# The Conformer convolution layer: projection in three one-pass products, and the depthwise convolution split between band matmuls on TensorE and taps on VectorE

## The reference, cut to what matters

```python
h = rms_norm(x, a_norm)
u = h @ w_in + b_in                       # 1024 -> 2048
a, gate = split(u, 2)
u = a * sigmoid(gate)
u = depthwise_causal_conv(u, w_dw) + b_dw # 31 taps in time, each channel by itself
u = silu(layer_norm(u, ln_g, ln_b))       # over the 1024 channels
x = x + u @ w_out + b_out
x = x + hierarchical_moe(rms_norm(x))     # then shared K/V, dilated attention, second MoE
```

## Time and profile before

| | us |
|---|---|
| median of 3 runs | 1848.68 (1848.21 to 1849.09) |
| the profiled execution's own time | 1853.51 |
| its span, first to last instruction | 1851.7 |
| TensorE, VectorE, ScalarE, GpSimd busy | 1562.5, 1170.6, 702.0, 509.6 |
| mean granted TensorE clock | 0.912 of full speed |

### The profile page before, as it was taken

How to read it: one execution, slowest core, us unless ns; L and a number is a source line. 1 busy time by engine, 2 the same in 40 slices (tenths; PEclk the granted TensorE clock), 3 DMA queues, 4 the chain that set the end, 5 groups by cost and what they waited for, 6 DMA issues and landing times. The chain is left out here.

```text
span 1851.7 us, 19289 instructions
## 1 busy us (share of the span) xinstructions
PE 1562.5 (84%) x6688; PEld 1171.9 (63%) x6688; DVE 1170.6 (63%) x1426; ACT 702.0 (38%) x762; POOL 509.6 (28%) x430
## 2 busy tenths in 40 slices
PE   6868048499999993799999999999998569999992
PEld 3323027367776662688888888888887556667760
DVE  2999992565666653848576574766643575656653
ACT  3323441245546551442232323323232335555541
POOL 2677700222222322314042240413310022322220
PEclk8988569589999996899999999999999679999996
DMA  3430000248887874212021211212111647888854
GB/s 151 188 136 21 25 0 30 114 162 356 356 364 324 341 310 186 93 58 70 32 81 55 68 57 45 79 45 69 55 57 70 288 150 294 343 371 350 368 228 158
DMA packets 44846, 303.08 MB, mean 164 GB/s; under 512 B 9488, under 2 KB 10256, under 8 KB 30992
## 3 DMA queue, kind: packets, MB, share of 16 engines
q1 hardware_dynamic: 34304, 284.98, 39.0%
q0 software_dynamic: 9648, 16.80, 2.5%
q10 hardware_dynamic: 864, 0.94, 0.1%
HBM read 295.34 MB, written 25.69 MB: 173 GB/s over the span
## 5 line engine op out<-in xcount | busy, mean ns | idle before, releaser
L626 POOL TENSOR_TENSOR KQ<-rope_ab 64x512 f32<-64x512 f32 x96 | 172.6, 1798 | 431.7 <-DVE rope_ab L1223 428.1
L1132 DVE TENSOR_TENSOR wgl<-WR,wgh 128x2048 fp32r<-128x2048 f32 x66 | 148.2, 2288 | 175.7 <-ACT wgh L741 172.8
L1404 PE MATMUL PS<-WR,SC 128*128 128x512 f32 x528 | 233.2, 594 | 4.1 <-ACT SC L775 3.2
L807 ACT ACTIVATE wh<-wraw 128x1024 fp32r<-128x1024 f32 x80 | 84.4, 1058 | 276.2 <-PE PS L1460 253.1
L1404 PEld LDWEIGHTS PS<-WR,SC 128*128 128x128 f32 x528 | 98.8, 190 | 118.3 <-issue 116.4
L1306 PE MATMUL PS<-HT,WR 128*128 128x512 f32 x256 | 123.5, 647 | 36.0 <-DVE SC L917 34.0
L928 DVE SCALAR_TENSOR_TENSOR SC<-SC 128x512 f32<-128x512 f32 x144 | 153.2, 1134 | 0.0
L1132 DVE TENSOR_TENSOR wul<-WR,wuh 128x2048 fp32r<-128x2048 f32 x66 | 148.0, 2283 | 0.3 <-ACT wuh L741 0.3
L741 ACT ACTIVATE wgh<-WR 128x2048 fp32r<-128x2048 f32 x66 | 122.4, 1904 | 62.0 <-DMA WR<-w_gate 62.0
L741 ACT ACTIVATE wuh<-WR 128x2048 fp32r<-128x2048 f32 x66 | 122.7, 1906 | 31.1 <-PE PS L1378 20.7
L1223 DVE TENSOR_TENSOR rope_ab<-PS,rope_sb 32x512 f32<-32x512 f32 x192 | 131.9, 687 | 2.6
(11 more groups left out here) (245 smaller groups left out, 3322.4 us busy)
## 6 DMA issues: line engine op xcount, KB each, us to landing
WR<-w_gate SPq DMA_DIRECT2D x33, 2048.0 KB, 12.3
WR<-w_up SPq DMA_DIRECT2D x33, 2048.0 KB, 16.8
WR<-w_down SPq DMA_DIRECT2D x33, 2048.0 KB, 14.0
wraw<-w_qkv SPq DMA_DIRECT2D x72, 512.0 KB, 3.3
WR<-w_in SPq DMA_DIRECT2D x8, 1024.0 KB, 4.8
WO<-w_out SPq DMA_DIRECT2D x1, 4096.0 KB, 14.8
xn_dram<-HTQ SPq DMA_DIRECT2D x8, 512.0 KB, 2.6
HT<-y_dram SPq DMA_DIRECT2D x8, 512.0 KB, 6.5
```

The source lines that it names most:

```text
L626: ins = nc.gpsimd.tensor_tensor(dst[h][0:HEAD, g, :], rope_ab[rows, 2 * (t % 2), :], rope_ab[rows, 2 * (t % 2) + 1, :], ALU.add)
L1132: V.tensor_tensor(lo[:, kts, :], raw[:, kts, :], hi[:, kts, :].bitcast(F32), ALU.subtract).then_inc(done, 1)
L1404: ins = M.matmul(PS[3 + h][:, :], hidT[:, ft, :], wd[b][:, ft, h * 512:(h + 1) * 512], start=ft == 0, stop=ft == FT - 1)
```

## The change

The projection's product is made from float32r halves: HTh and HTal (leading and trailing part of the normed x, all eight tiles), wih and wil (the same of a w_in tile; ScalarE `leading_in`, VectorE `trailing_in`). Each k-tile takes three products instead of one float32 product.

Time is stored "turned": the 512 tokens stand as 4 phases (PH) of 128, so that all shifts within a phase are shifts by whole columns. VectorE convolves channel tiles 0, 2 and 4 with all 31 taps; GpSimd takes no part. Tiles 1, 3, 5, 6, 7 go to TensorE: a matrix of 128x128 for each of 4 channel blocks and LAGS = 9 lags, 36 float32 products with 128 moving columns, in `convolve`. VectorE spreads the matrices from the taps (`spread`, 128x4608 elements). The partitions for this are 32 channels by 4 phases, so the gated tile goes to DRAM and comes back in four loads (`into_phases`), and the result the same way (`out_of_phases`), all issued by ScalarE. The order on all engines is written out. The loads of w_out and of the first experts' weights are issued after the projection and the taps, no longer between the w_in tiles, because their buffers hold the new tiles.

```diff
+PH = 4; CB = P // PH; TP = T // PH; LAGS = (CONV + PH - 2) // PH + 1
+BY_TAPS = (0, 2, 4)
+BY_BANDS = (1, 3, 5, 6, 7)
-CONV_COLS = C_WDW + KT * CONV
+CONV_COLS = C_WDW + len(BY_BANDS) * PH * LAGS * PH
...
 # SP
             for c in range(2, KT):
-                sp.wait_ge(u_mm[c % 2], c // 2)
+                sp.wait_ge(wil_done, c - 1)
                 sp.dma_start(w_in_sb[c % 2]..., a["w_in"][c])
-                if c == 2: expert_load(0, 1, 1, wg, "w_gate", wg_in)
-                if c in (3, 4): expert_load(0, c - 3, c - 3, wu, "w_up", wu_in)
-                if c == 6: sp.dma_start(WO[:, :, :], a["w_out"]).then_inc(wout_in, 16)
+            sp.wait_ge(u_mm, KT)
+            sp.wait_ge(taps_done, len(BY_TAPS))
+            sp.dma_start(WO[:, :, :], a["w_out"]).then_inc(wout_in, 16)
             expert_load(0, 0, 0, wg, "w_gate", wg_in)
+            expert_load(0, 0, 0, wu, "w_up", wu_in)
+            expert_load(0, 1, 1, wg, "w_gate", wg_in)
+            sp.wait_ge(silu_trail, KT)
+            expert_load(0, 1, 1, wu, "w_up", wu_in)
...
 # ScalarE
+                if k == "a":
+                    leading_in(0)
+                    for kt in range(KT):
+                        act.wait_ge(xT_ready.sem, xT_ready.at(k, kt + 1))
+                        nc.scalar.activation(turned(HTh[:, kt, :]), in_phases(PS[kt][:, :]), ACT.Copy, scale=...)
+            def leading_in(c):
+                act.wait_ge(win_in[c % 2], (c // 2 + 1) * 16)
+                if c >= 2: act.wait_ge(u_mm, c - 1)
+                nc.scalar.activation(wih[c % 2][:, :, :, :], w_in_sb[c % 2], ACT.Copy)
-            def products(b, i, ahead): ...
+            def into_phases(c):
+                act.wait_ge(glu_done, c + 1)
+                act.dma_start(u_dram[c], ug[n % 2]).then_inc(ug_out, 16)
+                act.wait_ge(ug_out, 16 * (n + 1))
+                if n >= 2: act.wait_ge(conv_mm, n - 1)
+                there = u_dram[c].rearrange("(q c) (s t) -> s c q t", q=PH, s=PH)
+                for s in range(PH):
+                    act.dma_start(uph[n % 2][s * CB:(s + 1) * CB, :, LAGS - 1:], there[s])
+            def out_of_phases(c):
+                act.wait_ge(yph_done, n + 1)
+                act.dma_start(c_dram[c], yph[n % 2]).then_inc(yph_out, 16)
+                act.wait_ge(yph_out, 16 * (n + 1))
+                for q in range(PH):
+                    act.dma_start(HTQ[q * CB:(q + 1) * CB, c, :]..., back[q])
+            leading_in(1); sigmoid(0); leading_in(2); sigmoid(1); into_phases(1)
+            leading_in(3); sigmoid(2); leading_in(4); sigmoid(3); into_phases(3)
+            leading_in(5); out_of_phases(1); sigmoid(4); leading_in(6); sigmoid(5); into_phases(5)
+            leading_in(7); out_of_phases(3); sigmoid(6); into_phases(6); out_of_phases(5)
+            sigmoid(7); into_phases(7); out_of_phases(6); out_of_phases(7)
...
 # VectorE
+                elif k == "a":
+                    trailing_in(0)
+                    for kt in range(KT):
+                        V.scalar_tensor_tensor(turned(HTal[:, kt, :]), in_phases(PS[kt][:, :]), vn[...],
+                                               turned(HTh[:, kt, :].bitcast(F32)), ALU.mult, ALU.subtract)
+            def trailing_in(c):
+                V.tensor_tensor(wil[c % 2][:, :, :, :], w_in_sb[c % 2], wih[c % 2][...], ALU.subtract)
+            trailing_in(1); spread(1); spread(3); gated(0); trailing_in(2)
+            taps(0, 0, 10); gated(1); trailing_in(3); taps(0, 10, CONV); tapped(0); gated(2)
+            trailing_in(4); taps(2, 0, 12); gated(3); biased(1); trailing_in(5); spread(5)
+            taps(2, 12, CONV); tapped(2); gated(4); biased(3); trailing_in(6)
+            taps(4, 0, 6); gated(5); spread(6); trailing_in(7); taps(4, 6, 10); gated(6)
+            taps(4, 10, 20); biased(5); spread(7); taps(4, 20, 25); gated(7)
+            taps(4, 25, CONV); tapped(4); biased(6); biased(7)
...
 # GpSimd
-            with pool.Fori(0, KT // 2) as i: ...    # the 10 additions of each tile
...
 # TensorE
+            def project_in(c):
+                pe.wait_ge(wil_done, c + 1)
+                if c >= 2: pe.wait_ge(glu_done, c - 1)
+                for s in range(2):
+                    for kt in range(KT):
+                        M.matmul(dst, wih[b][:, kt, s, :], HTh[:, kt, :], ...)
+                        M.matmul(dst, wih[b][:, kt, s, :], HTal[:, kt, :], ...)
+                        M.matmul(dst, wil[b][:, kt, s, :], HTh[:, kt, :], ...)
+            def convolve(c):
+                pe.wait_ge(uph_in[n % 2], (n // 2 + 1) * PH * 16)
+                if n >= 2: pe.wait_ge(yph_done, n - 1)
+                for q in range(PH):
+                    for m in range(LAGS):
+                        M.matmul(PS[6 + n % 2][:, q * TP:(q + 1) * TP], band[n % 2][:, q, m, :],
+                                 uph[n % 2][:, q, LAGS - 1 - m:LAGS - 1 - m + TP], ...)
+            project_in(0); project_in(1); project_in(2); convolve(1); project_in(3); project_in(4)
+            convolve(3); project_in(5); project_in(6); convolve(5); project_in(7); convolve(6); convolve(7)
```

More of the change, by code:

```diff
@@ L677, in _ @@
             act.wait_ge(cvec_in, 16)
[L679 to L708, removed]
+            def sigmoid(c):
+                act.wait_ge(u_mm, c + 1)
+                if c >= 2:
+                    act.wait_ge(glu_done, c - 1)
+                nc.scalar.activation(sig[c % 2], PS[2 * (c % 2) + 1][:, :], ACT.Sigmoid,
+                                     bias=cv[:, C_BIN + KT + c:C_BIN + KT + c + 1]).then_inc(sig_done, 1)
@@ new lines, in taps @@
+            def taps(c, first, last):
+                w = C_TAP + BY_TAPS.index(c) * (CONV + 1)
+                for t in range(first, last):
+                    tap, win = cv[:, w + t:w + t + 1], upad[:, t:t + T]
+                    if t == 0:
+                        dve.wait_ge(glu_done, c + 1)
+                        steps.mark(V.tensor_scalar(accv[0], win, tap, cv[:, w + CONV:w + CONV + 1], ALU.mult, ALU.add))
+                    elif t == 1:
+                        steps.mark(V.tensor_scalar(accv[1], win, tap, None, ALU.mult))
+                    else:
+                        steps.wait(1)
+                        steps.mark(V.scalar_tensor_tensor(accv[t % 2], win, tap, accv[t % 2], ALU.mult, ALU.add))
@@ new lines, in _ @@
+            dve.wait_ge(conv_init, 4)
+            trailing_in(1)
+            spread(1)
+            spread(3)
+            gated(0)
+            trailing_in(2)
+            taps(0, 0, 10)
+            gated(1)
+            trailing_in(3)
+            taps(0, 10, CONV)
+            tapped(0)
+            gated(2)
+            trailing_in(4)
+            taps(2, 0, 12)
+            gated(3)
+            biased(1)
+            trailing_in(5)
+            spread(5)
+            taps(2, 12, CONV)
@@ L945, in _ @@
+            tapped(2)
+            gated(4)
+            biased(3)
+            trailing_in(6)
+            taps(4, 0, 6)
+            gated(5)
+            spread(6)
+            trailing_in(7)
+            taps(4, 6, 10)
+            gated(6)
+            taps(4, 10, 20)
+            biased(5)
+            spread(7)
+            taps(4, 20, 25)
+            gated(7)
+            taps(4, 25, CONV)
+            tapped(4)
+            biased(6)
+            biased(7)
             dve.wait_ge(mean_mm, 1)
@@ new lines, in _ @@
+            project_in(0)
+            project_in(1)
+            project_in(2)
+            convolve(1)
+            project_in(3)
+            project_in(4)
+            convolve(3)
+            project_in(5)
+            project_in(6)
+            convolve(5)
+            project_in(7)
+            convolve(6)
+            convolve(7)
+            pe.wait_ge(conv_init, 4)
+            order = (0, 1, 2, 3, 5, 4, 6, 7)
+            for c in order:
+                if c in BY_TAPS:
+                    pe.wait_ge(taps_done, BY_TAPS.index(c) + 1)
+                else:
+                    n = BY_BANDS.index(c)
+                    pe.wait_ge(conv_in[n % 2], (n // 2 + 1) * PH * 16)
+                ins = M.matmul(PS[4][:, :], onesf, HTQ[:, c, :], start=c == order[0], stop=c == order[-1])
@@ L1629, in lay_out @@
     by_tile = lambda v: v.reshape(-1, P).T
+    w_dw = f["a_w_dw"][0]
+    bands = np.zeros((PH, CB, KT, PH, LAGS, PH), np.float32)
+    for s in range(PH):
+        for m in range(LAGS):
+            for r in range(PH):
+                if 0 <= PH * m + r - s < CONV:
+                    bands[s, :, :, :, m, r] = w_dw[CONV - 1 - (PH * m + r - s)].reshape(KT, PH, CB).transpose(2, 0, 1)
+    taps = cat([cat([w_dw.reshape(CONV, KT, P)[:, c].T, f["a_b_dw"][0].reshape(KT, P)[c][:, None]], 1) for c in BY_TAPS], 1)
+    by_block = np.tile(f["a_b_dw"][0].reshape(KT * PH, CB).T, (PH, 1))
+    same = np.tile(np.eye(CB, dtype=np.float32), (PH, 1))
     a = {"x": f["x"]}
```

256 lines of the change are left out of this document (145 added, 111 removed).

## The result

The changed kernel takes 1800.41 us (median of 4 runs, 1799.73 to 1800.69) against 1848.85 (4 runs, 1848.21 to 1849.09): ratio 0.9738, 95% interval 0.9721 to 0.9755. It is 48.4 us faster; 1792, or 56.3 off, was forecast. The value lies in the range, with 8.4 us missing. The profiled execution took 1800.69 us, its span is 1798.3.

What follows compares the result with a forecast made beforehand. VectorE, hindered by GpSimd's additions, was taken to bound the convolution stage. Start 30.2, work 131.8 and stalls 14.3 give 176.3; the first square moves from 250.9 to 194.6, 56.3 us off: 1792 (forecast 1778 to 1798, range 1778 to 1815).

Steps and rivals of the forecast that it cites:

- The start: Before the projection: scaling, trailing part and eight HTal tiles let TensorE start at 30.2 us instead of 23.49.
- TensorE's rates: Projection and bands: 10.9 us per project tile, 2.6 for the slow start, 8.4 per band tile, 131.8 in all.
- Rival 3: Band stretches run at the low clock, 16.8 us a tile: 27 us saved, 1822; chance 0.07.
- rival 4: VectorE is not quickened, taps stay at the mean 1.134 us: 18 us saved, 1830; chance 0.05.
- Crossings in an idle queue: Moves into and out of the phases: store and landing 2.6 us each, four issues 1.8.
- Rivals 2 and 5: Every store and landing slow: 2, at 6.2 us, 36 saved, 1812, chance 0.12; 5, at 14.3, 53 lost, 1902, chance 0.03.
- The stalls: TensorE waits before convolve(3), project_in(6), convolve(5) and convolve(7): 3.3, 4.4, 1.3 and 5.3 us, 14.3 together.
- The end of the stage: After the last band at 176.3: last tile back at 191.7, mean matmul to 193.8, first square at 194.6 us.
- WOh: ScalarE's eight w_out copies before the squares, 7.67 us, end at 193.2 and stay hidden.
- From the first square to the output projection: Subtraction, squares and variance as before: 17.8 us to the first output product.
- The rest: Behind the first square all stays as before; expert weights, landing at about 187, cost nothing.
- Rival 1: Four-element-step operands (HTal, gated and tapped of tap tiles) at 1.7 times: 7 us later, 49 saved, 1799; chance 0.10.

Runs made afterwards that it cites:

- before_dve_only: The kernel before with all 31 taps of every tile on VectorE, no products on ScalarE and no additions on GpSimd: 1825.78 us.
- late_experts: The changed kernel with the three expert weight loads issued only after the last crossing, w_out staying where it is: 1785.30 us.
- sp_late: late_experts with all crossings but the last two moved from ScalarE's queue to SP's: 1773.30 us.
- split_last: The changed kernel with ScalarE making the eight WOh tiles between the last tile's store and its loads: 1797.67 us.
- sp_crossings: The changed kernel with crossings on SP's queue as in sp_late, but the expert loads right behind w_out as in the changed kernel: 1789.90 us.
- late_experts_again: The kernel of late_experts measured once more, on the same chip and in the same rounds as sp_late: 1785.40 us.
- f32_late: late_experts with the projection in float32 again, one product per k-tile and no leading or trailing parts: 1790.95 us.
- late_w_out: The changed kernel with w_out as well as the three expert loads issued behind the last crossing: 1795.96 us.

## Why the prediction was right, and what its sum had wrong

The mechanism was right: the stage was VectorE's with GpSimd in its way, the work went to TensorE, and the gain stands at the first square (48.8 us there, 48.4 in the medians). Two things in the nearness of the numbers are luck. The forecast had 6.3 us too many up to the last band and 13.8 too few behind it, which in part cancel. And the 48.8 and 48.4 agree more closely than the traces do: these are 47.0 us apart at the first output product (268.66 and 221.63), 49.3 at the first copy of an expert weight (347.07 and 297.78) and 53.4 at their ends, the profiled execution of the kernel before being 4.8 above its median. By one of the prediction's own signs, a first square set by WOh, the end of the stage went wrong. Point by point:

- *The start.* Forecast 30.2, measured 29.50. `trailing_in(0)` beside GpSimd took 4.44 us (4.8 forecast), the eight HTal tiles 5.34 (5.9).
- *TensorE's rates.* A project tile takes 10.88 us (54.06 to 64.94 between two of ScalarE's sigmoids; 10.9 forecast). The first 12 products came at 0.43 apart, then 0.23, so 2.4 for the slow start (2.6). The prediction put that down to the lower clock; the clock row reads 1.00 over these products all the same (29.50 to 64.70), so that cause is not shown. A band tile takes 8.2 to 8.3 at a granted clock of 1.00 (8.4 forecast). Rival 3, the low clock in the bands, is out.
- *VectorE's taps.* 21 of them take 14.0 us, 0.667 each; rival 4 is out, and before_dve_only, with the rows beside it, shows the cause.
- *Crossings in an idle queue.* The stores land in 2.0 to 2.1 us, the loads in 2.0 (2.6 forecast, bounds 2.3 to 3.3). Rivals 2 and 5, 6.2 or 14.3 for each, are out.
- *The stalls.* Forecast 3.3, 4.4, 1.3 and 5.3, 14.3 in all; measured 1.1, 6.0, 0 and 0. The one in front of `project_in(6)` is the chain that the forecast told: ScalarE stands in line for a crossing's store, so `leading_in(5)` and `trailing_in(5)` come 5.5 us late, and 19 taps follow. late_experts still has this stall, and sp_late, which differs from it only in that line, has none. What the walk left out is that such a stall also costs some 3 us by the lower clock behind it. The 5.3 in front of `convolve(7)` did not come: that tile's loads were issued from 157.50 to 159.26 and took 2.1, so they were all but through when w_out was issued at 160.61. The last band ended at 170.0 instead of 176.3.
- *The end of the stage: the term that was mis-sized.* The prediction gave the last tile "store 0.45 + 6.2, four issues 1.8, landing 6.2". The store took 20.9 with its issue, the four issues 1.8 and the last landing 2.1, so 24.8 stood where 14.65 was charged, 10.1 us too few. (The store was also issued 1.0 later after the last band than forecast, because ScalarE was still issuing tile 6's loads, until 171.70.) The 6.2 came from a small load at the start of the kernel. The prediction had the 25 us of the 10 MB in hand and did not let the store wait for them. In seven runs the last store landed 0.4 to 1.1 us behind the last of the big loads issued ahead of it, and in an eighth with none ahead in 2.1:

| kernel | in flight | last of it landed | store issued | landed |
|---|---|---|---|---|
| changed | 10 MB | 192.1 | 171.74 | 192.6 |
| split_last | 10 MB | 191.5 | 171.02 | 192.0 |
| sp_crossings | 10 MB | 182.0 | 161.57 | 182.4 |
| late_experts | 4 MB | 175.1 | 170.51 | 176.2 |
| late_experts_again | 4 MB | 175.0 | 170.39 | 176.0 |
| f32_late | 4 MB | 183.0 | 178.37 | 183.9 |
| sp_late | 4 MB | 165.7 | 160.90 | 166.8 |
| late_w_out | none | | 170.50 | 172.6 |

- *WOh.* Said to be hidden until 193.2. ScalarE could not begin it while it stood behind the store, so 2.7 us of it came onto the path (mean complete at 198.6, first square at 202.07 as the last copy ended, where 0.8 was forecast). split_last, where WOh is made during the store, had its first square 3.9 us sooner.
- *From the first square to the output projection.* 17.8 forecast, 19.6 measured (221.63). The 16 variance matmuls took 10.5 us instead of 9.2, at a clock of 0.71 instead of 0.82, and the SiLU, now with its four-element step, 1.31 instead of 0.80.
- *The rest.* No expert weight came late, neither here nor with the loads 18 us later. "As before" did not hold quite: between the output projection and the first expert the 64 narrow matmuls of 20 columns took 11.46 us instead of 13.10 (clock 0.61 instead of 0.53), part of the 2.3 us that the traces win back there.

The sum again: -6.3 (bands end earlier), +1.0 (the store issued later), +10.1 (last crossing), +2.7 (WOh), 7.5 us later at the first square than 194.6.

Rival 1, strided operands, held in part. Groups of VectorE by form, with and without the four-element step, 25 to 215 us:

```profile
L944 DVE SCALAR_TENSOR_TENSOR HTal<-PS,vn,HTh 128x512 fp32r<-128x512 f32 x7 | 4.7, 734 | 0.0
L979 DVE SCALAR_TENSOR_TENSOR SC<-PS,SC 128x512 f32<-128x512 f32 x5 | 3.8, 751 | 3.2 <-ACT SC L695 3.2
L1004 DVE TENSOR_TENSOR SC<-PS,SC 128x512 f32<-128x512 f32 x5 | 3.4, 690 | 8.8 <-PE PS L1423 8.8
L979 DVE SCALAR_TENSOR_TENSOR taps_sb<-PS,SC 128x512 f32<-128x512 f32 x3 | 3.4, 1139 | 2.6 <-ACT SC L695 2.6
L996 DVE TENSOR_TENSOR HTQ<-taps_sb 128x512 f32<-128x512 f32 x3 | 3.2, 1072 | 0.1
```

The gated product into a tap tile takes 1139 ns against 751 (1.5 times), the tapped one 1072 against 690 for a plain sum of the same size. HTal, which takes PSUM apart in phases, stays at 734. So the step costs 0.4 us in six instructions of VectorE and 0.5 in each SiLU, not the 7 us of the rival. Its rule, that accesses on a new cache line each time are penalised, is in the Trainium skill (Advanced Engine Details and Errata, SBUF Cachelines); the trace agrees for these SBUF operands.

What is not settled: why the queues served the small store so late. The store before it, issued 2.2 us behind w_out, took 7.1 us in the changed kernel while 10 MB were on their way, so it did not wait for all of them. The Trainium skill (DMA: Bandwidth & Descriptors, Queues, rings and completion order) says that an engine takes its queues in turn, a packet from each. Served so, a store of 256 KB would not have to wait for 10 MB, and the table speaks against it for stores issued 9 us or more behind the loads. Nor does a run part the store from the four loads just ahead of it in ScalarE's own queue, which were held as long. No run here tells what the queue looked like inside.

## What to carry to other kernels

When a rewrite sets free several buffers at once, ask what their loads, all issued in the same microsecond, will be in front of: one small store on the path can cost as much as all of them together, and a wait on the loads that have cover costs one line (15 us here). A queue that both computes and carries a store, a wait and loads passes every transfer's latency on to whoever needs its next instruction; put such hops on a queue with nothing to compute (12 us here in the medians, 9 at the first square). And before work is spread over one more engine, try it without that engine: the kernel before, with all taps given back to VectorE, gained half as much as the whole change.

The fastest version run is sp_late at 1773.3 us, 76 below the kernel before and 27 below the changed one.

## What the runs showed of the hardware that was not expected

- A 256 KB store beside other queues' loads: 2.1 us with nothing in flight, 5.65 with 4 MB issued 11.5 us ahead, 20.9 with 10 MB issued 11.1 us ahead. Four 64 KB loads 9 us behind the 10 MB took 17.6, in an idle queue 2.0.
- GpSimd's 128x512 additions made VectorE's SBUF multiply-adds 2.1 times as long (1.40 against 0.667 us), so its help was worth nothing. The product HTal, which reads PSUM and one operand in SBUF, took 0.67 us beside its additions and after them.
- A stall of TensorE costs more than itself: after 6.0 us of waiting the granted clock was 0.50 for 4 us and 0.81 over the next 5, 2.9 us of work lost.
